# A two-layer hybrid encoder on one core: four DeltaNet batches prepared together, with the 16x16 blocks inverted on VectorE

## What is computed

```python
a_mat = jnp.where(strict, jnp.einsum("nbhid,nbhjd->nbhij", k_beta, k) * decay, 0.0)
lhs = a_mat + jnp.eye(DN_CHUNK, dtype=jnp.float32)
value = lax.linalg.triangular_solve(lhs, v_beta, left_side=True, lower=True, unit_diagonal=True)
k_cumdecay = lax.linalg.triangular_solve(lhs, k_beta * jnp.exp(gc)[..., None],
                                         left_side=True, lower=True, unit_diagonal=True)
qk = jnp.einsum("nbhid,nbhjd->nbhij", q, k) * decay

def step(state, xs):
    q_i, k_i, value_i, kcd_i, qk_i, gc_i = xs
    v_new = value_i - kcd_i @ state
    out = (q_i * jnp.exp(gc_i)[..., None]) @ state + qk_i @ v_new
    g_last = gc_i[..., -1]
    k_w = k_i * jnp.exp(g_last[..., None] - gc_i)[..., None]
    state = state * jnp.exp(g_last)[..., None, None] + jnp.einsum("bhcd,bhce->bhde", k_w, v_new)
```

## Time and profile before

| what | value |
|---|---|
| median of three runs | 1958.35 us |
| profiled execution, its own time | 1958.37 us |
| its span in the trace | 1956.6 us |
| TensorE busy | 1910.0 us, 98% of the span |
| TensorE weight load busy | 1636.8 us, 84% |
| VectorE, ScalarE, GpSimd busy | 1475.7, 1125.5, 130.1 us |
| mixer, layer 0 and layer 1 | about 139 to 334 us, and about 712 to 893 us |

### The profile page before, as it was taken

One profiled execution on the slowest core, in us unless ns is written; L12 is line 12 of the kernel. 1 busy time (PEld: TensorE's weight loads), 2 busy tenths in 40 slices (PEclk: granted clock), 3 DMA queues, 4 the chain that ended last, 5 costly groups with the idle time before them and its releaser, 6 DMA issues.

```text
span 1956.6 us, 27474 instructions
## 1 busy us (share of the span) xinstructions
PE 1910.0 (98%) x11150; PEld 1636.8 (84%) x11150; DVE 1475.7 (75%) x1812; ACT 1125.5 (58%) x1249; POOL 130.1 (7%) x119
## 2 busy tenths in 40 slices
PE   9998999999999989999999999999999999999998
PEld 8987768999999978789788888888888888888886
DVE  8758666555549656656788988888889798888886
ACT  5634424433335633334677777677776777777775
POOL 1015041000000014050000000000000000000000
PEclk9998999999999989999999999999999999999999
DMA  7400002544443100024699999999999899999994
GB/s 299 148 28 1 1 33 79 200 177 174 161 171 132 63 28 1 1 86 153 234 355 355 349 352 359 343 352 351 353 365 353 331 356 356 359 349 370 355 362 177
DMA packets 64196, 443.58 MB, mean 227 GB/s; under 512 B 8172, under 2 KB 8204, under 8 KB 13632
## 3 DMA queue, kind: packets, MB, share of 16 engines
q1 hardware_dynamic: 62032, 437.87, 59.8%
q0 software_dynamic: 1760, 3.78, 0.6%
q10 hardware_dynamic: 272, 0.10, 0.0%
HBM read 440.66 MB, written 2.17 MB: 226 GB/s over the span
## 4 chain that ended last, share of the span: by engine, by line
PE 89%; DVE 8%; issue 1%; ACT 1%; DMA 0%; POOL 0%; SPq 0%; DVEq 0%; POOLq 0%; ACTq 0%
PE ps L1936 23%; PE ps L1938 23%; PE ps L1937 23%; PE ps L2363 2%; PE ps L2348 2%; PE ps L1949 2%; PE ps L2367 2%; DVE w_lo L1208 2%; DVE cacc L1300 2%; PE ps L2547 1%; PE ps L2174 1%; PE ps L2558 1%; PE ps L2221 1%; PE ps L2315 1%; PE ps L2259 1%
## 5 line engine op out<-in xcount | busy, mean ns | idle before, releaser
L1265 DVE TENSOR_TENSOR m_lo<-raw,m_hi 128x2048 fp32r<-128x2048 f32 x336 | 768.5, 2290 | 135.7 <-ACT m_hi L851 135.6
L851 ACT ACTIVATE m_hi<-raw 128x2048 fp32r<-128x2048 f32 x336 | 644.1, 1918 | 268.9 <-PE ps L1938 268.9
L1936 PE MATMUL ps<-m_hi,xe_hi 128*128 128x512 f32 x896 | 358.5, 400 | 0.0
L1938 PE MATMUL ps<-m_lo,xe_hi 128*128 128x512 f32 x896 | 353.6, 395 | 0.0
L1937 PE MATMUL ps<-m_hi,xe_lo 128*128 128x512 f32 x896 | 353.6, 395 | 0.0
L1208 DVE TENSOR_TENSOR w_lo<-raw,w_hi 128x1024 fp32r<-128x1024 f32 (+1 forms) x164 | 183.3, 1156 | 105.6 <-ACT w_hi L816 105.6
L1936 PE MATMUL ps<-u_hi,w_hi 128*128 128x272 f32 x800 | 235.2, 294 | 6.6 <-DVE w_lo L1208 4.5
L1938 PE MATMUL ps<-u_lo,w_hi 128*128 128x272 f32 x800 | 231.5, 289 | 0.0
L1937 PE MATMUL ps<-u_hi,w_lo 128*128 128x272 f32 x800 | 230.4, 288 | 0.0
L816 ACT ACTIVATE w_hi<-raw 128x1024 fp32r<-128x1024 f32 (+1 forms) x164 | 159.5, 1002 | 114.9 <-PE ps L1938 106.0
L1938 PEld LDWEIGHTS ps<-m_lo,xe_hi 128*128 128x128 f32 x896 | 168.0, 187 | 41.1
(11 more groups left out here) (397 smaller groups left out, 2777.1 us busy)
## 6 DMA issues: line engine op xcount, KB each, us to landing
raw<-in_moe_units SPq DMA_DIRECT2D x336, 1024.0 KB, 4.9
raw<-in_dense_units SPq DMA_DIRECT2D x57, 1024.0 KB, 4.8
raw<-in_dense_units SPq DMA_DIRECT2D x16, 768.0 KB, 5.5
raw<-in_dense_units SPq DMA_DIRECT2D x8, 896.0 KB, 4.5
w_uq<-in_mla_w_uq SPq DMA_DIRECT2D x2, 768.0 KB, 4.6
mats<-in_c_mats POOLq DMA_DIRECT2D x1, 1216.0 KB, 10.5
h<-in_h_rows SPq DMA_DIRECT2D x2, 544.0 KB, 4.6
bias_rows<-bias_row POOLq DMA_DIRECT2D x1, 1088.0 KB, 25.3
```

The source lines that it names most:

```text
L851: nc.scalar.activation(m_hi[k % RING][:, :], raw[:, slot, :], ACT.Copy).then_inc(m_hi_ready, 1)
L1265: V.tensor_tensor(m_lo[k % RING][:, :], raw[:, mslot(k), :], m_hi[k % RING][:, :].bitcast(F32), ALU.subtract).then_inc(m_lo_ready, 1)
L1936: mm(o, w[0], x[0], start=first, stop=False)
L1938: return mm(o, w[0], x[1], start=False, stop=last)
```

## The change

The four batches of a layer are prepared together, ahead of both steps of the recurrence. Levels 0 to 3 of the doubling, which invert the 16x16 blocks on the diagonal, are no longer done by masks and matmuls. In their place TensorE transposes A of the backward batches (`ai`), VectorE gathers all the diagonal blocks into a tile of its own by 32x32 transposes (`blocks_in`), inverts them there in three steps with products and reductions (`blocks_level`), and puts them back by transposes (`blocks_out`) into a tile that GpSimd has cleared (`zero`); TensorE transposes the result (`ot`) and ScalarE copies it out, so that both T and TT are there. Levels 4, 5 and 6 stay as they were, but for four batches in one loop. The turns of the attention groups are dealt out anew: eleven stand in the preparation, 18 in the three levels, five in each step of the recurrence. The column sums of the gates are made once, in `delta_parts`, into `dcol`; `diff` adds a mask of -1e30 in the same instruction that subtracts, so the masked product `pt_tri` is gone. Ten idle products of TensorE ahead of the second step are gone. SyncE's load of the first unit of the output projection waits for the step `state` of TensorE instead of GpSimd's `vb`, and the second for `pt` instead of `pt_tri`.

```diff
+M_NEG = M_LV + LEVELS
+BASE = 4
+BLOCK = 1 << BASE
...
+        batch = {}
+        for s in range(2):
+            for d in range(2):
+                batch[s, d] = {"AT": dn_a1[:, s] if d else dn_a[:, s, 0], "M": dn_m[:, s, d],
+                               "T": dn_o[:, s, 1] if d else dn_t0[:, s], "TT": dn_a[:, s, 1] if d else dn_o[:, s, 0],
+                               "X": dn_x[:, s, d], "DT": dn_dt[:, s, d], "PT": dn_dt[:, s, d], "QE": dn_qe[s][:, d],
+                               "Vb": dn_a1[:, s] if d else dn_vb[:, s], "KW": k_tok[:, d],
+                               "RT": dn_m[:, s, d] if s else row_g0[:, d], "RB": row_beta[:, d] if s else row_b0[:, d]}
...
+        def packed(q):
+
+            return slice(32 * q, 32 * q + 32)
+
+        def diagonal(x, q):
+
+            return x[packed(q)].rearrange("p s d h n -> p (s d h) n")[:, :, packed(q)].rearrange("p g (b i) -> p i b g", b=2)
...
-                        dn_pool.wait(sp, l, "vb", 1, 1)
+                        dn_pe.wait(sp, l, "state", 0, 1)
                     if u == out_units[l][1]:
-                        dn_pool.wait(sp, l, "pt_tri", 1, 1)
+                        dn_pool.wait(sp, l, "pt", 1, 1)
...
+                dn_dve.wait(pool, l, "gate_cols")
+                rows(0)
+                dn_pe.wait(pool, l, "rows", 0, 0)
+                rows(1)
+                S.mark(nc.gpsimd.memset(dn_o[:, :, :, :, :].rearrange("p s d h n -> p (s d h n)"), 0.0), "zero")
+                masks(BASE)
+                dn_dve.wait(pool, l, "qk", 1)
+                for s, d in BATCHES:
+                    product(batch[s, d]["PT"], qk[:, (s, 1 - s)[d]], batch[s, d]["DT"], "pt", s, d)
+                queries(0)
+                for n in range(BASE + 1, LEVELS):
+                    masks(n)
+                S.wait(pool, l, "mask", 1, LEVELS - 1, 1)
+                for s, d in BATCHES:
+                    t = (s, 1 - s)[d]
+                    product(batch[s, d]["Vb"], v_tok[:, t], bc(gcol[:, t, 1, 4 * d:4 * d + 4], 2, P), "vb", s, d)
+                dn_act.wait(pool, l, "expcols")
+                for d in range(2):
+                    product(batch[0, d]["KW"], k_tok[:, d], bc(dcol[:, 2, d, 4 * d:4 * d + 4], 2, P), "kw", 0, d)
+                queries(1)
...
+                def turned_a(s):
+                    pe_w("ai", s)
+                    S.mark(nc.scalar.activation(dn_a[:, s, 1], heads(ps[:, 2 - s, :]), ACT.Copy), "ai", s)
+
+                def turned_block(s, d):
+                    pe_w("ot", s, d)
+                    S.mark(nc.scalar.activation(batch[s, d]["TT" if d else "T"], heads(ps[:, 2 * d + s, :]), ACT.Copy), "ot", s, d)
...
+                def diff(s, d):
+                    t = (s, 1 - s)[d]
+                    pe_w("rows", s, d)
+                    for hh in range(H):
+                        i = V.scalar_tensor_tensor(batch[s, d]["DT"][:, hh], ps[:, 2 * d, P * hh:P * hh + P],
+                                                   dcol[:, 0, t, 4 * d + hh:4 * d + hh + 1], mat(M_NEG + d), ALU.subtract, ALU.add)
+                    S.mark(i, "diff", s, d)
+
+                def prod(s, d):
+                    B = batch[s, d]
+                    act_w("decay", s, d)
+                    link(V.tensor_tensor(B["AT"], kk[:, (s, 1 - s)[d]], B["DT"], ALU.mult))
+                    pe_w("beta", s, d)
+                    S.mark(V.tensor_tensor(B["AT"], B["AT"], heads(ps[:, 1, :]), ALU.mult), "prod", s, d)
+
...
+                def blocks_in():
+                    act_w("ai", 1)
+                    for q in range(4):
+                        i = V.transpose(blk[packed(q), :, :], diagonal(dn_a, q))
+                    link(i)
+                    link(V.tensor_scalar(blk_r[:, :, :], blk[:, :, 0:BLOCK], pick[0], None, ALU.mult))
+                    V.memset(blk_u[:, :, :], 0.0)
+                    u = blk_u[:, :, :].rearrange("p i j -> p (i j)")
+                    link(V.scalar_tensor_tensor(blk_r[:, :, :], blk[:, :, BLOCK:2 * BLOCK], pick[1], blk_r[:, :, :], ALU.mult, ALU.add))
+                    V.memset(u[:, 0:256:17], 1.0)
+                    link(V.tensor_copy(u[:, 16:256:34], blk_r[:, :, :].rearrange("p i j -> p (i j)")[:, 16:256:34]))
+
+                def blocks_level(size):
+                    nb = BLOCK // (2 * size)
+                    cube = blk_tmp[:, 0:nb * size ** 3].rearrange("p (b r c k) -> p b r c k", b=nb, r=size, c=size)
+                    x = blk_x[:, 0:nb * size ** 2].rearrange("p (b r c) -> p b r c", b=nb, r=size)
+                    left = blocks_of(blk_r, size, 0, size, (BLOCK, 0, 1))
+                    low = blocks_of(blk_u, size, size, size, (BLOCK, 0, 1))
+                    high = blocks_of(blk_u, 0, 0, size, (0, 1, BLOCK))
+                    made = blocks_of(blk_u, size, 0, size, (BLOCK, 1))
+                    x_in = bass.AP(x.tensor, x.offset, [x.ap[0], [size * size, nb], [0, size], [1, size], [size, size]])
+                    parts = [np.s_[:, :, r] for r in range(size)] if size <= nb else [np.s_[:, b] for b in range(nb)]
+                    for at_ in parts:
+                        i = V.tensor_tensor(cube[at_], left[at_], high[at_], ALU.mult)
+                    link(i)
+                    link(V.tensor_reduce(blk_x[:, 0:nb * size ** 2], cube.rearrange("p b r c k -> p (b r c) k"), AX.X, ALU.add))
+                    for at_ in parts:
+                        i = V.tensor_tensor(cube[at_], low[at_], x_in[at_], ALU.mult)
+                    link(i)
+                    for at_ in parts:
+                        i = V.tensor_reduce(made[at_], cube[at_], AX.X, ALU.add)
+                    link(i)
+
+                def blocks_out():
+                    for b in range(2):
+                        i = V.tensor_scalar(blk_e[:, :, BLOCK * b:BLOCK * b + BLOCK], blk_u[:, :, :], pick[b], -1.0, ALU.mult, ALU.mult)
+                    link(i)
+                    dn_pool.wait(dve, l, "zero")
+                    for q in range(4):
+                        i = V.transpose(diagonal(dn_o, q), blk_e[packed(q), :, :])
+                    S.mark(i, "blocks")
...
+                diff(0, 0)
+                diff(0, 1)
+                turns(1)
+                prod(0, 0)
+                diff(1, 0)
+                prod(0, 1)
+                turns(1)
+                meta_level(0)
+                diff(1, 1)
+                prod(1, 0)
+                turns(1)
+                prod(1, 1)
+                meta_level(1)
+                turns(1)
+                blocks_in()
+                turns(1)
+                blocks_level(2)
+                meta_level(2)
+                turns(1)
+                blocks_level(4)
+                turns(1)
+                meta_level(3)
+                blocks_level(8)
+                turns(1)
+                blocks_out()
+                turns(1)
+                meta_level(4)
+                pe_w("m_state")
+                V.tensor_copy(state[:, 0:4, :], heads(ps[:, 0, :]))
+                S.mark(V.tensor_copy(state[:, 4:8, :], heads(ps[:, 1, :])), "m_state")
+                turns(1)
+                for n in range(BASE, LEVELS):
+                    turns(3)
+                    for s in range(2):
+                        for d in range(2):
+                            B, bank = batch[s, d], 2 * d + s
+                            pe_w("up", s, n, d)
+                            if n < LEVELS - 1:
+                                t_c = level_cols(B["T"], n, d)
+                                V.tensor_tensor(t_c, t_c, ps[:, bank, H * P // 2:H * P].rearrange("p (c i) -> p c i", i=1 << n), ALU.subtract)
+                            t_c = level_cols(B["TT"], n, 1 - d)
+                            i = V.tensor_tensor(t_c, t_c, ps[:, bank, 0:H * P // 2].rearrange("p (c i) -> p c i", i=1 << n), ALU.subtract)
+                            S.mark(i, "T", s, n, d)
+                        turns(1 + s)
...
+                rows(0, 0)
+                rows(0, 1)
+                beta(0, 0)
+                turns(1)
+                rows(1, 0)
+                dve_w("qk", 1)
+                meta_x(0)
+                beta(0, 1, 0, 0)
+                turns(1)
+                rows(1, 1)
+                beta(1, 0, 0, 1)
+                meta_x(1)
+                turns(1)
+                meta_up(1)
+                beta(1, 1, 1, 0)
+                turn_a(0)
+                turns(1)
+                turn_a(1)
+                meta_x(2)
+                turns(1)
+                meta_up(2)
+                turns(1)
+                meta_x(3)
+                turns(1)
+                meta_up(3)
+                turns(1)
+                dve_w("m_T", 3)
+                S.mark(mm(ps[:, 3, 0:P], X["TT"], X["Vb"], start=True, stop=True), "m_vnew")
+                turns(1)
+                act_w("m_vnew")
+                S.mark(mm(ps[:, 3, P:2 * P], X["X"], X["PT"], start=True, stop=True), "m_out")
+                act_w("ai", 1)
```

(37 more changed lines are left out.)

479 lines of the change are left out of this document (196 added, 283 removed).

## The result

The changed kernel takes **2070.36 us** (median of 4 runs, 2066.40 to 2076.68) against 1958.68 before: ratio 1.0573, interval [1.0541, 1.0606]. It is 112 us slower where 26 us faster was forecast, so the forecast and its range were wrong. The times of runs are medians; one of e8's four executions fell in a slower state of the chip (2086.21 us) and is left out.

A forecast was written before the change was run, and what follows sets the result against it. TensorE was taken to bound the kernel, except one VectorE-paced stretch per layer. 61.5 us removed or moved out, 17.1 + 16.5 + 1.6 added: 26.3 less than 1958.37, so 1932 us, range 1908 to 1953.

The forecast's parts named there:

- What bounds the kernel now: Whole kernel: TensorE holds 89% of the chain, VectorE 8%; in the mixer VectorE paces one stretch per layer, TensorE the rest.
- What is removed, 31.0 and 26.9: Second pair's preparation: TensorE work and idle time removed or moved out, 31.0 us in layer 0, 26.9 in layer 1.
- the sum: Both mixers: 61.5 us removed or moved out, 17.1 + 16.5 + 1.6 added, 26.3 us less.
- What the first stretch becomes, 69.0 and 73.0: Preparation of four batches, paced by VectorE: 69.0 us in layer 0 against 51.9, 73.0 in layer 1 against 56.5.
- GpSimd's 3: Preparation: GpSimd's ten products running beside VectorE cost 3 us, bounds 0 and 8.
- the other waits: Preparation in layer 0: VectorE's waits for TensorE and ScalarE and the lower clock, within 20.5 us of waits including GpSimd's.
- The rest: Levels 4 to 6 and recurrence: same TensorE work reordered, copies and subtractions covered, else about 1 us a level; 1.6 added.
- Rival 4: Block inversion: VectorE's transposes, at 2.5 us each instead of 0.62, add 30 us; 1962 us in all. Chance 0.08.
- Rival 3: Preparation: turns keep their 7.2 us pitch, making it 82 us in both layers; nothing gained, 1958 us. Chance 0.09.
- Rival 5: Behind the preparation: a hold-up (bare step 1 at the lower clock, weights' loads), 5 to 15 us over forecast. Chance 0.06.
- a chain in levels 4 to 6 that is VectorE's: Sign of being wrong: in levels 4 to 6 the chain would be VectorE's; no size given.
- Transposes above 1 us: Sign of being wrong: VectorE's transposes in the block inversion taking above 1 us, where 0.62 was assumed.

The follow-up runs named there:

- e8: The kernel before, with VectorE's attention turns one more ahead from level 1 of the first pair on: 2057.3 us, ratio 1.0483.
- e11: Changed kernel, VectorE one turn earlier from the block inversion, ScalarE from level 4, six GpSimd products earlier, level 6 masks on VectorE: 1930.6 us.
- e13: Changed kernel with only one more turn on VectorE ahead of the block inversion and one more on ScalarE ahead of level 4: 1970.6 us.
- e14: The kernel before, VectorE and ScalarE each leaving out one turn ahead of level 1 of the first pair: 2131.9 us, ratio 1.0915.
- e5: Changed kernel with ten idle TensorE products ahead of the sums in five norm turns of each layer: 2061.7 us, ratio 1.0519.

## Why the prediction was wrong, by its own steps

- **What bounds the kernel now**: right in what it read (the chain is TensorE's) and blind to why: TensorE had no gaps there because the other engines stood one turn ahead.
- **What is removed, 31.0 and 26.9**: right in TensorE's work. Behind level 4 it is busy for 23.3 and 28.9 us less in e11 than before (111.4 and 89.9 for 134.7 and 118.8), where the sum had 28.7 and 27.0 with `m_state`; in layer 0 e11's clock is lower, 0.96 for 0.99. With the leads and GpSimd repaired (e11) the mixers take 182.2 and 162.7 against 190.8 and 180.6, 26.5 us less in all; the sum said 26.3. That agreement is partly luck, closer than its terms: e11 is 3 and 6 us shorter than forecast in the preparation and, behind it, 10 longer in layer 0 and 1 shorter in layer 1.
- **What the first stretch becomes, 69.0 and 73.0**: measured 75.8 and 77.4. The mis-sized term is the transposes, 0.62 us each and 1.035 measured (3.3 us a layer). The rest of the inversion was forecast at 7.9 and sums to 7.9. In layer 0 VectorE is busy for 54.3 us, where the list and GpSimd's 3 gave 51.5, and idle for 21.5, where the other waits gave 17.5. TensorE's wait of 6.1 at 171 to 177 us, for the inversion's first part in front of a turn, is the missing lead again; e11 takes the stretch to 66.1 and 66.9.
- **"The rest": the step that failed.** "ScalarE's copies and VectorE's subtractions are covered", since turns stand between `x` and `up`; "the same TensorE work in another order". The work is the same (461 and 463 matmul records from level 4 to `ks` in the changed kernel and in e11), but it took 103 and 77 us. I looked at what stands between two steps on TensorE and not at how many turns stand ahead of the same step on the other two engines. Priced there were about 1 us a level if the cover went; found were 79 and 48 us. Of these 127, 79 go with the leads (e13) and 40 with GpSimd's edits (e11 against e13), and e11 itself is 9 over the forecast. Against e11 they split into 72 us of TensorE work at the lower clock and 47 of idle time, over both layers (152.4 busy and 32.8 idle against 111.4 and 4.7 in layer 0; 120.7 and 24.7 against 89.9 and 5.9 in layer 1).
- **GpSimd**: contention was priced in the preparation, at 3 us, and called free behind it ("under 20 us of a level"). It is there that it costs 40 us over both layers, most of it as work at the lower clock. Beside it many of VectorE's instructions take about as long as one product of GpSimd, 1.2 us, though each is shorter alone: 1.47 for 0.50, 1.51 for 0.43, 1.03 for the 0.30 of a cast. That agrees with the Trainium skill, page "SBUF — State Buffer", section "Who interferes with whom", by which the second to come blocks until the first is done. The cast has one input, so the part on two SBUF inputs that the prediction used doesn't cover it. The rule was cited for the products of the inversion, and should have been read against every place where the change puts GpSimd's list.
- **The rivals**: none was it. Rival 4 had the transposes at 2.5 us; they take 1.035. Rival 3's 82 us of preparation was not reached. Rival 5, a hold-up behind the preparation, had the place and a tenth of the size, for other reasons: the weights' loads don't show.
- **What would show it**: "a chain in levels 4 to 6 that is VectorE's" was named as a sign of being wrong, and it came in part: in layer 0 the chain is VectorE's from 256 to 271.5 us, and goes back and forth between the two engines in the ring. "Transposes above 1 us" came too, at 1.035, and was worth 3.3 us a layer. Nothing in the text gave the first more than about 1 us a level.

Left open: why e14 loses 175 us and the changed kernel, with the same leads missing, only some 100 of its loss by them. In e14 the twelve levels of a layer's two pairs run without a lead, in the changed kernel the three of its four batches; that this is the whole difference wasn't tried.

## What to carry to other kernels

Where several engines walk one list of shared turns, count for every step how many turns stand ahead of it on each engine, before and after a change; the distance is part of the schedule, although no diff line shows it. Here one is right. None costs 5% of the whole kernel (the changed one against e13) and 9% (e14), and two on VectorE alone 5% (e8). Price a rule on two engines' interference at each place where either list moves, not only where the new code stands.

## What the runs showed of the hardware

- VectorE's transpose of fp32, 32x512, takes 1.035 us, 1.5 times its 128x512 product (0.68). Reading the diagonal blocks and writing packed, and the reverse, take the same.
- Even a very small VectorE instruction can be held for about one GpSimd product: a product of 88x1 took 1.21 us (166.12 in e11) for 0.15, and a cast with one input 1.03 for 0.30. Not all are: in the same stretch of e11 (164.7 to 170 us) the instructions that read scores from PSUM kept their 0.43 to 0.44, and a reciprocal of 88x2 its 0.15.
- A busy TensorE doesn't mean that its clock is back. In the changed kernel it stayed at 0.50, its lower level, from 268 to 302 us, with a wait of 6.0 and then 2.9 in every 14.8. In e13 it stayed at 0.50 from 251 to 280 with no wait in between; in e11 the same turns ran at 1.00. Idle products in the waits of the changed kernel brought 0.98 from 268 to 302 (e5) and gave back 9 us of 2070; the leads, which remove the waits, gave 100.
